# Memory values copied by two engines in halves, and a new order of VectorE, ScalarE and GpSimd work at the middle boundary of a two-block transformer kernel

## The chip, the cores and the metric

The kernel runs on one core of a Trainium2 chip. A core has TensorE (PE) for matmuls, VectorE (DVE), ScalarE (ACT) and GpSimd (POOL) for everything else, SyncE (SP) for issuing transfers; products land in PSUM, which the kernel uses as eight banks of 128 x 512 floats. The metric is the device time of one execution in microseconds; the median of three runs before the change is 2526.79 us.

## The reference

Two blocks follow each other on 256 tokens of width 2048. What matters here is how one ends and the other begins, and the memory attention in the first.

```python
def mem_cross_attention(x, mem, w_q, w_kv, w_o):
    q = (x @ w_q).reshape(B, S, N_HEADS_MEM, HEAD_DIM)
    k, v = jnp.split(mem @ w_kv, 2, axis=-1)
    s = jnp.einsum('bshd,bmhd->bhsm', q, k) * (HEAD_DIM ** -0.5)
    p = jax.nn.softmax(s, axis=-1)
    o = jnp.einsum('bhsm,bmhd->bshd', p, v).reshape(B, S, MEM_WIDTH)
    return o @ w_o

def first_block(x, mem, ...):
    ...
    y = mem_cross_attention(x, mem, w_q_mem, w_kv_mem, w_o_mem)
    x = layer_norm(ALPHA * x + y, ln_g[1], ln_b[1])
    y = swiglu(x, w_ffn_in, w_ffn_out)
    return layer_norm(ALPHA * x + y, ln_g[2], ln_b[2])

def second_block(x, c, ...):
    mod = jax.nn.silu(c) @ w_ada + b_ada
    h = modulate(rms_norm_2(x, norm1_w), shift1, scale1)
    p = h @ w_in
    ...
```

At the middle boundary the rows of x therefore pass through a layer norm (first root), and their result through an RMS norm (second root), before the first product of the second block, `lstm_q`, can begin.

## The kernel before

All weights come as one stream of 1 MB tiles through four buffers `raw`. ScalarE rounds each half tile to `whi`, VectorE subtracts to get `wlo`, and TensorE makes three matmuls for each product (hi x hi, hi x lo, lo x hi), at line 2215 with weights stationary, at 2219, 2258 and 2305 with the tokens stationary. TensorE is thus fed by ScalarE and VectorE with two halves in hand; each engine works strictly through its own instruction list, which is written out by hand, and waits on counting semaphores.

**Memory values.** The product `v_mem` fills one pair of PSUM banks: bank t holds the 128 memory rows of tile t and 512 columns, 128 for each of four heads. ScalarE waits for the product's end (`weights_used`) and copies both banks to `vm` in one instruction (line 757, by `read_out_rows`). TensorE waits for it (`pair_read`), and then multiplies `vm` by the transposed scores of each head (`mem_pT`) at line 2525; ScalarE and VectorE split the four results into `shi` (line 1032) and `slo` (line 1766) for the next product `o_mem`. VectorE's half tile at line 1521 stands ahead of the `slo`.

**The middle boundary.** `down1` ends with row tile 0's four banks, then row tile 1's (`last_four`). For each bank of 512 columns VectorE adds the residual and sums (`add_bank`, line 1620), and ScalarE squares and sums (`edge_square`, 670). From the sums come mean, variance and, by ScalarE's `root` (701) and VectorE's four small steps of `scale_from_root` (1675 to 1682), a scale. VectorE multiplies by `gamma` (`widen`, 1838) and then scales and adds `beta` (`normalise`, 1845). ScalarE squares the normed rows (`normed_squares`, 682), VectorE makes their mean (`mean_square`, 1664 to 1669), and a second root and scale follow. Row tile 0 is scaled by ScalarE (`scaled_rows`, 696), row tile 1 by VectorE (1833). Both are needed by TensorE's transposes (2155), then `lstm_q` begins (2215). While TensorE has nothing to do it multiplies a block of ones (`keep_busy`, 2143): 51 such matmuls here, of 512 columns, that nobody reads.

The counts tell which step is meant: `edge_var` and `edge_root` count 3 and 4 for row tile 0's two roots, 5 and 6 for row tile 1's. `scale_ready` counts every scale that VectorE has made, in the order in which it makes them. GpSimd, at the boundary, starts two transfers (572, 573), sets two tiles (574, 575) and makes four triangular masks (580) as soon as `down1` is done; they are needed by the gates and the heads of `lstm`, well into the second block.

## Time and profile before

| | us |
|---|---|
| median of three runs (2526.73 to 2526.83) | 2526.79 |
| the profiled execution | 2526.35 |
| its span, first to last instruction | 2524.7 |
| TensorE busy in it | 2504.4 |
| VectorE, ScalarE, GpSimd busy | 1670.4, 1247.2, 107.6 |
| memory values, `v_mem` to `o_mem` | 719.0 to 723.5 |
| middle boundary, end of `down1` to start of `lstm_q` | 1473.3 to 1487.7 |

The profile is of one execution. A timeline row gives start and duration in us from the span's start, the engine, the line of the kernel, the operation, the tile written and those read, shape, and the number of instructions that the row merges; a bracket tells how long the engine was idle before and what released it. Since engines overlap, what counts is which chain of waits sets TensorE's next start. A TensorE that is busy with the blocks of ones counts as busy in the table and does nothing for the result.

### The profile page before, as it was taken

What the parts mean: (1) busy time and instruction counts of PE and PEld (TensorE: products, weight loads), DVE (VectorE), ACT (ScalarE), POOL (GpSimd) and SP (SyncE); (2) the same over time, 40 slices, a digit from 0 to 9 for tenths busy, and PEclk for the clock granted to TensorE, in tenths of its full rate; (3) what the DMA queues carried; (4) which work ended last, traced back from release to release, by engine and by line L of the source; (5) the groups of instructions that cost most, each with busy time, mean ns of one, the idle gap of its engine ahead of it and who ended that gap; (6) DMA issues with size and microseconds to landing.
All of it is one profiled execution on the core that took longest, in us unless ns stands there. A gap on an engine that the chain in (4) does not pass through costs nothing.

```text
span 2524.7 us, 45946 instructions
## 1 busy us (share of the span) xinstructions
PE 2504.4 (99%) x17995; PEld 2327.2 (92%) x17999; DVE 1670.4 (66%) x2084; ACT 1247.2 (49%) x1588; POOL 107.6 (4%) x151
## 2 busy tenths in 40 slices
PE   9999999999999999999999999999999999999998
PEld 9799999998979999999988878988899999998886
DVE  5564675467867777777777775575766666665556
ACT  5444554444564444344444464545655555554444
POOL 0000000000100000000122000000000000000000
PEclk9999999999999999999999999999999999999999
DMA  7455445569647888888978736445455555555553
GB/s 304 154 199 186 157 146 193 187 256 362 256 157 299 332 344 329 343 330 339 363 285 330 259 135 214 167 149 216 167 187 197 193 190 199 186 196 209 190 198 118
DMA packets 82066, 581.95 MB, mean 230 GB/s; under 512 B 9308, under 2 KB 9468, under 8 KB 12096
## 3 DMA queue, kind: packets, MB, share of 16 engines
q1 hardware_dynamic: 65232, 462.98, 50.0%
q0 software_dynamic: 14464, 104.23, 10.6%
q10 hardware_dynamic: 2288, 13.59, 1.3%
q8 instruction: 58, 0.95, 0.2%
q14 instruction: 24, 0.20, 0.0%
HBM read 578.64 MB, written 2.12 MB: 230 GB/s over the span
## 4 chain that ended last, share of the span: by engine, by line
PE 96%; DVE 2%; issue 1%; ACT 1%; POOL 0%; DVEq 0%; ACTq 0%; POOLq 0%
PE ps L2215 60%; PE ps L2258 23%; PE ps L2219 7%; PE ps L2305 3%; PE ps L2283 0%; PE ps L2155 0%; PE ps L2576 0%; PE ps L2143 0%; PE ps L2417 0%; POOL small L539 0%; DVE wlo L1249 0%; PE ps L2450 0%; PE ps L2462 0%; DVE res L1838 0%; DVE res L1845 0%
## 5 line engine op out<-in xcount | busy, mean ns | idle before, releaser
L1249 DVE TENSOR_TENSOR wlo<-raw,whi 128x1024 fp32r<-128x1024 f32 x853 | 1034.0, 1227 | 659.8 <-ACT whi L633 655.9
L633 ACT ACTIVATE whi<-raw 128x1024 fp32r<-128x1024 f32 x850 | 891.3, 1060 | 961.2 <-PE ps L2215 595.0
L2215 PE MATMUL ps<-xhi,whi 128*128 128x256 f32 x4176 | 1155.4, 277 | 1.8 <-issue 1.8
L2215 PE MATMUL ps<-xhi,wlo 128*128 128x256 f32 x4176 | 1149.8, 275 | 0.0
L2215 PE MATMUL ps<-xlo,whi 128*128 128x256 f32 x4176 | 1149.6, 275 | 0.0
L2215 PEld LDWEIGHTS ps<-xhi,whi 128*128 128x128 f32 x4176 | 784.1, 188 | 4.0 <-issue 3.2
L2215 PEld LDWEIGHTS ps<-xlo,whi 128*128 128x128 f32 x4176 | 784.2, 188 | 0.4
L2215 PEld LDWEIGHTS ps<-xhi,wlo 128*128 128x128 f32 x4176 | 784.0, 188 | 0.0
L1313 DVE SCALAR_TENSOR_TENSOR ada<-ada,cb 128x2048 f32<-128x2048 f32 x96 | 219.5, 2286 | 2.7 <-DMA ada<-in_w_ada 2.7
L2258 PE MATMUL ps<-wlo,dhi 128*128 128x512 f32 x624 | 192.2, 389 | 0.0
L2258 PE MATMUL ps<-whi,dlo 128*128 128x512 f32 x624 | 192.1, 389 | 0.0
L2258 PE MATMUL ps<-whi,dhi 128*128 128x512 f32 x624 | 192.0, 389 | 0.0
L2258 PEld LDWEIGHTS ps<-whi,dlo 128*128 128x128 f32 x624 | 117.1, 188 | 24.5
L2258 PEld LDWEIGHTS ps<-wlo,dhi 128*128 128x128 f32 x624 | 117.1, 188 | 24.3
L2258 PEld LDWEIGHTS ps<-whi,dhi 128*128 128x128 f32 x624 | 117.1, 188 | 24.1
L2219 PE MATMUL ps<-whi,xhi 128*128 128x512 f32 (+1 forms) x224 | 87.9, 392 | 0.0
L2219 PE MATMUL ps<-whi,xlo 128*128 128x512 f32 (+1 forms) x224 | 85.8, 383 | 0.0
L2219 PE MATMUL ps<-wlo,xhi 128*128 128x512 f32 (+1 forms) x224 | 85.8, 383 | 0.0
L554 POOL DMA_DIRECT2D ada<-in_w_ada x94 | 50.2, 534 | 808.5 <-DVE ada L1313 790.7
L2073 DVE SCALAR_TENSOR_TENSOR conv<-ps,col,conv 128x255 f32<-128x255 f32 x176 | 72.7, 475 | 17.2 <-ACT conv L1182 17.2
L2215 PE MATMUL ps<-ohi,whi 128*128 128x256 f32 x256 | 70.6, 276 | 0.1
L2215 PE MATMUL ps<-ohi,wlo 128*128 128x256 f32 x256 | 70.4, 275 | 0.0
(374 smaller groups left out, 2179.0 us busy)
## 6 DMA issues: line engine op xcount, KB each, us to landing
raw<-in_stream SPq DMA_DIRECT2D x435, 1024.0 KB, 4.8
ada<-in_w_ada POOLq DMA_DIRECT2D x96, 1024.0 KB, 6.7
raw<-in_stream SPq DMA_DIRECT2D x5, 512.0 KB, 9.3
mem_part<-in_memt ACTq DMA_DIRECT2D x2, 1024.0 KB, 6.7
res<-in_x ACTq DMA_DIRECT2D x1, 2048.0 KB, 12.7
gamma<-in_ln_g ACTq DMA_DIRECT2D x2, 1024.0 KB, 9.8
beta<-in_ln_b ACTq DMA_DIRECT2D x2, 1024.0 KB, 14.0
gate_row<-gate_store POOLq DMA_DIRECT2D x2, 1024.0 KB, 7.7
```

The costliest lines, as they stand in the source:

```text
L554: pool.dma_start(ada[s % 2][:], w_ada[at(n0 + s, i, per)]).then_inc(ada_landed[s % 2], 16)
L633: act.activation(whi[:, h % 4], raw[g % 4][:, 1024 * half:1024 * half + 1024], ACT.Copy)\
L1249: dve.tensor_tensor(wlo[:, h % 4], raw[g % 4][:, 1024 * half:1024 * half + 1024], whi[:, h % 4].bitcast(F32), ALU.subtract).then_inc(lo_re ...
L1313: dve.scalar_tensor_tensor(out=ada[slot][:], in0=ada[slot][:], scalar=1.0, in1=cb[:], op0=ALU.mult, op1=ALU.mult, accum_out=mod[:, bass.ds ...
L2073: ins = dve.scalar_tensor_tensor(out=conv[:, q, S * m + to:S * m + to + S - 1], in0=bank[:, S * m + fro:S * m + fro + S - 1], scalar=col[: ...
L2215: ins = pe.matmul(o, w[:, k, P * m:P * m + P], a(kt), start=begins and n == 0 and m % 2 == 0, stop=ends and n == 2, skip_group_check=True)
L2219: ins = pe.matmul(o, a(kt)[:, P * m:P * m + P], w[:, k, :], start=begins and n == 0, stop=ends and n == 2, skip_group_check=True)
L2258: ins = pe.matmul(ps[:, 4 * t + 2 * half + n], a[:, s, P * t:P * t + P], w[:, h % 4, 512 * n:512 * n + 512], start=first and a is hi and w ...
L2305: return pe.matmul(ps[:, 4 * t + n], a[:, s, P * t:P * t + P], w[:, 512 * (n % 2):512 * (n % 2) + 512], start=begins and s == 0 and m == 0 ...
```

## The change

It has two parts. First, `vm` is copied by two engines, each one bank (one tile of memory rows), each in two halves of two heads: ScalarE makes `vm[:, 0]`, VectorE `vm[:, 1]`, placed behind VectorE's rest of the last weight tile and ahead of its half tile for `o_mem`. TensorE waits for the first halves ahead of head 0 and for the second halves ahead of head 2.

Second, at the middle boundary, VectorE takes row tile 1's third bank ahead of row tile 0's second mean square, and its fourth bank ahead of row tile 0's second scale; that scale moves behind row tile 1's `normalise`. ScalarE squares row tile 1's second and third bank ahead of row tile 0's second root and waits for the fifth scale, where it waited for the fourth, ahead of `scaled_rows`. The rest of the first weight half is made in two quarters. GpSimd's transfers and masks wait until row tile 1's scaled rows are done (`chunk_ready[1]` at 8), and the 51 matmuls on ones become 46.

```diff
@@ GpSimd
             pool.wait_ge(weights_used, through(AT["lstm_q"] - 1))
+            pool.wait_ge(chunk_ready[1], 8)
             pool.dma_start(dftc[:], dft).then_inc(late_landed, 16)
@@ ScalarE
-            read_out_rows(CH["v_mem"], g0 + 3, vm[:])
+            act.wait_ge(weights_used, through(g0 + 3))
+            c = CH["v_mem"]
+            act.activation(vm[:, 0, 0:S], ps[:, 2 * (c % 2), 0:S], ACT.Copy).then_inc(first_vm, 1)
+            act.activation(vm[:, 0, S:2 * S], ps[:, 2 * (c % 2), S:2 * S], ACT.Copy).then_inc(pair_read[c % 2], 1)
             wide_start("o_mem")
@@ ScalarE, middle boundary
             normed_squares(0)
+            edge_squares(1, 1, 1, 3)
             root(0, 4)
-            edge_squares(1, 1, 1, 4)
+            edge_squares(1, 1, 3, 4)
             second_upper_of_next(g0)
             root(1, 5)
-            scaled_rows(4)
+            scaled_rows(5)
             normed_squares(1)
@@ VectorE
-            def scale_from_root(t, count):
+            def scale_from_root(t, count, scaled=None):
...
-                dve.wait_ge(scale_ready, count)
+                dve.wait_ge(scale_ready, count if scaled is None else scaled)
@@ VectorE, memory values
             rest(g0 + 4)
+            dve.wait_ge(weights_used, through(g0 + 3))
+            c = CH["v_mem"]
+            for d in range(2):
+                dve.tensor_copy(vm[:, 1, S * d:S * d + S], ps[:, 2 * (c % 2) + 1, S * d:S * d + S]).then_inc(second_vm, 1)
             more_rest("o_mem", 1, (0,))
@@ VectorE, middle boundary
+            def rest_of_quarter(g, quarter):
+
+                cols = slice(512 * quarter, 512 * quarter + 512)
+                dve.wait_ge(hi_ready, 2 * g + 1)
+                return dve.tensor_tensor(wlo[:, 2 * g % 4, cols], raw[g % 4][:, cols], whi[:, 2 * g % 4, cols].bitcast(F32), ALU.subtract)
...
             add_bank(1, 1, 1, g0 - 1)
+            add_bank(1, 1, 2, g0 - 1)
             mean_square(0, 17)
-            scale_from_root(0, 4)
-            add_bank(1, 1, 2, g0 - 1)
             add_bank(1, 1, 3, g0 - 1)
             mean(1, 1)
             widen(1, 0, 13)
+            off_centre(1)
             widen(1, 1, 18)
-            off_centre(1)
             centred_variance(1, 20)
-            widen(1, 2, 20)
-            scale_from_root(1, 5)
+            widen(1, 2, 19)
+            scale_from_root(1, 5, 4)
             widen(1, 3, 20)
             normalise(1)
-            rest(g0, halves=(0,))
+            scale_from_root(0, 4, 5)
+            rest_of_quarter(g0, 0)
+            rest_of_quarter(g0, 1).then_inc(lo_ready, 1)
             mean_square(1, 24)
@@ TensorE
-            pe.wait_ge(pair_read[CH["v_mem"] % 2], reads(CH["v_mem"]))
+            pe.wait_ge(first_vm, 1)
+            pe.wait_ge(second_vm, 1)
             for h in range(HEADS_MEM):
+                if h == 2:
+                    pe.wait_ge(pair_read[CH["v_mem"] % 2], reads(CH["v_mem"]))
+                    pe.wait_ge(second_vm, 2)
                 pe.wait_ge(m_pT, h + 1)
...
-            first_chunk(4, "lstm_q", xn, 17, 51)
+            first_chunk(4, "lstm_q", xn, 17, 46)
```

What stands in a row at the places that the prediction speaks of follows. In these rows `ps` is PSUM, `edge` the small sums and scales, `res` the residual rows, `xn` the scaled rows, and a bracket names the semaphores that an instruction waits for.

VectorE at the middle boundary, from row tile 1's second bank on, before:

```order
L1620 SCALAR_TENSOR_TENSOR res,edge<-res,ps 128x512 [waits bank_done]
L1664 TENSOR_REDUCE edge<-edge 128x1 [waits edge_sq]
L1666 TENSOR_SCALAR edge<-edge 128x1 [waits dve_order]
L1669 SCALAR_TENSOR_TENSOR edge<-edge 128x1 [waits edge_sq,dve_order]
L1675 TENSOR_SCALAR edge<-edge 128x1 [waits edge_var]
L1677 RECIPROCAL edge<-edge 128x1 [waits edge_root]
L1679 SCALAR_TENSOR_TENSOR edge<-edge 128x1 [waits dve_order]
L1682 SCALAR_TENSOR_TENSOR edge<-edge 128x1 [waits dve_order]
L1620 SCALAR_TENSOR_TENSOR res,edge<-res,ps 128x512 [waits bank_done,scale_ready]
L1627 TENSOR_REDUCE edge<-edge 128x1 [waits added]
L1620 SCALAR_TENSOR_TENSOR res,edge<-res,ps 128x512 [waits weights_used]
```

The same place now:

```order
L1627 SCALAR_TENSOR_TENSOR res,edge<-res,ps 128x512 [waits bank_done] x2
L1634 TENSOR_REDUCE edge<-edge 128x1 [waits added]
L1671 TENSOR_REDUCE edge<-edge 128x1 [waits edge_sq]
L1673 TENSOR_SCALAR edge<-edge 128x1 [waits dve_order]
L1676 SCALAR_TENSOR_TENSOR edge<-edge 128x1 [waits edge_sq,dve_order]
L1627 SCALAR_TENSOR_TENSOR res,edge<-res,ps 128x512 [waits weights_used]
```

The third bank moved ahead of the mean square, and the four small steps of the scale are gone from in front of the fourth bank.

VectorE at the end of row tile 1's first norm, before:

```order
L1845 SCALAR_TENSOR_TENSOR res<-res,edge,beta 128x512 [waits dve_order]
L1845 SCALAR_TENSOR_TENSOR res<-res,edge,beta 128x512 x3
L1249 TENSOR_TENSOR wlo<-raw_50,whi 128x1024 [waits hi_ready]
L1664 TENSOR_REDUCE edge<-edge 128x1 [waits edge_sq]
L1666 TENSOR_SCALAR edge<-edge 128x1 [waits dve_order]
```

And now:

```order
L1862 SCALAR_TENSOR_TENSOR res<-res,edge,beta 128x512 [waits dve_order]
L1862 SCALAR_TENSOR_TENSOR res<-res,edge,beta 128x512 x3
L1682 TENSOR_SCALAR edge<-edge 128x1 [waits edge_var]
L1684 RECIPROCAL edge<-edge 128x1 [waits edge_root]
L1686 SCALAR_TENSOR_TENSOR edge<-edge 128x1 [waits dve_order]
L1689 SCALAR_TENSOR_TENSOR edge<-edge 128x1 [waits dve_order]
L1845 TENSOR_TENSOR wlo<-raw_50,whi 128x512 [waits hi_ready,scale_ready]
L1845 TENSOR_TENSOR wlo<-raw_50,whi 128x512 [waits hi_ready]
L1671 TENSOR_REDUCE edge<-edge 128x1 [waits edge_sq]
L1673 TENSOR_SCALAR edge<-edge 128x1 [waits dve_order]
```

Row tile 0's second scale, the four rows from L1682, now stands behind the four rows of `normalise`.

ScalarE at the middle boundary, from row tile 0's normed squares on, before:

```order
L682 ACTIVATE ps,edge<-res 128x512 [waits normed0] x4
L701 ACTIVATE edge<-edge 128x1 [waits edge_var]
L670 ACTIVATE ps,edge<-res,edge 128x512 [waits added] x3
L706 ACTIVATE whi<-raw_50 128x1024 [waits weights_used]
L701 ACTIVATE edge<-edge 128x1 [waits edge_var]
L696 ACTIVATE xn<-res,edge 128x512 [waits scale_ready]
L696 ACTIVATE xn<-res,edge 128x512 x3
L682 ACTIVATE ps,edge<-res 128x512 [waits normed1] x4
L701 ACTIVATE edge<-edge 128x1 [waits edge_var]
```

And now:

```order
L685 ACTIVATE ps,edge<-res 128x512 [waits normed0] x4
L673 ACTIVATE ps,edge<-res,edge 128x512 [waits added] x2
L704 ACTIVATE edge<-edge 128x1 [waits edge_var]
L673 ACTIVATE ps,edge<-res,edge 128x512 [waits added]
L709 ACTIVATE whi<-raw_50 128x1024 [waits weights_used]
L704 ACTIVATE edge<-edge 128x1 [waits edge_var]
L699 ACTIVATE xn<-res,edge 128x512 [waits scale_ready]
L699 ACTIVATE xn<-res,edge 128x512 x3
L685 ACTIVATE ps,edge<-res 128x512 [waits normed1] x4
L704 ACTIVATE edge<-edge 128x1 [waits edge_var]
```

The first root moved behind two squares; the scaled rows still stand ahead of row tile 1's normed squares.

## Rows read from the trace of the kernel before

**Rows 1.** The profile's page, part 1: busy time, share of the span, instructions.

```profile
PE 2504.4 (99%) x17995; PEld 2327.2 (92%) x17999; DVE 1670.4 (66%) x2084; ACT 1247.2 (49%) x1588; POOL 107.6 (4%) x151
```

**Rows 2.** Waits of TensorE over the span: total us, times, longest.

```profile
PE ps L2155 <- DVE xn L1833: 2.6, 2, 1.4
...
PE ps L2215 <- DVE small L1592: 1.6, 1, 1.6
...
PE ps L2525 <- ACT vm L757: 1.1, 1, 1.1
```

**Rows 3.** Timeline of the memory values, start us, us, engine, line, operation.

```profile
719.01 1.02 ACT L757 ACTIVATE vm<-ps 128x1024 f32<-128x1024 f32 x1 [2.15 <-PE ps L2219]
...
720.09 3.72 PE L2525 MATMUL ps<-mem_pT,vm 128*128 128x256 f32 x16 [1.11 <-ACT vm L757]
721.01 1.23 DVE L1521 TENSOR_TENSOR more_lo<-raw,more_hi_o_mem 128x1024 fp32r<-128x1024 f32 x1 [6.15 <-ACT more_hi_o_mem L917]
721.26 0.38 ACT L1032 ACTIVATE shi<-ps 128x256 fp32r<-128x256 f32 x1 [0.28 <-PE ps L2525]
```

**Rows 4.** Groups by line and shape: busy us, mean ns of one, idle before.

```profile
L1344 DVE COPY ckv<-ps 128x512 f32<-128x512 f32 x1 | 0.7, 680 | 0.0
...
L1147 ACT ACTIVATE fa_late<-ps 128x256 f32<-128x256 f32 x4 | 1.5, 376 | 4.1 <-PE ps L2615 4.1
```

**Rows 5.** Timeline of VectorE over the middle boundary.

```profile
1466.08 0.15 DVE L1644 TENSOR_TENSOR edge<-edge 128x1 f32<-128x1 f32 x1
...
1466.97 0.68 DVE L1620 SCALAR_TENSOR_TENSOR res<-res,ps 128x512 f32<-128x512 f32 x1
...
1473.98 0.68 DVE L1620 SCALAR_TENSOR_TENSOR res<-res,ps 128x512 f32<-128x512 f32 x1
...
1474.95 1.42 DVE L1838 SCALAR_TENSOR_TENSOR res<-res,edge,gamma 128x512 f32<-128x512 f32 x2
1476.28 0.35 DVE L1644 TENSOR_TENSOR edge<-edge 128x1 f32<-128x1 f32 x1
...
1477.60 0.74 DVE L1838 SCALAR_TENSOR_TENSOR res<-res,edge,gamma 128x512 f32<-128x512 f32 x1
1478.26 0.14 DVE L1675 TENSOR_SCALAR edge<-edge 128x1 f32<-128x1 f32 x1
...
1478.96 0.75 DVE L1838 SCALAR_TENSOR_TENSOR res<-res,edge,gamma 128x512 f32<-128x512 f32 x1
...
1482.40 1.22 DVE L1249 TENSOR_TENSOR wlo<-raw,whi 128x1024 fp32r<-128x1024 f32 x1
...
1483.91 0.16 DVE L1669 SCALAR_TENSOR_TENSOR edge<-edge 128x1 f32<-128x1 f32 x1
...
1484.98 1.67 DVE L1833 TENSOR_SCALAR xn<-res,edge 128x512 f32<-128x512 f32 x4
```

**Rows 6.** Timeline of ScalarE over the same stretch.

```profile
1477.82 2.54 ACT L696 ACTIVATE xn<-res,edge 128x512 f32<-128x512 f32 x4
1480.53 0.60 ACT L682 ACTIVATE ps<-res 128x512 f32<-128x512 f32 x1 [0.16 <-DVE res L1845]
...
1483.05 0.19 ACT L682 ACTIVATION_READ_ACCUMULATOR ps<-res 128x1 f32 x1
```

**Rows 7.** Timeline of GpSimd over the same stretch: its four masks.

```profile
1475.80 1.67 POOL L580 TENSOR_SCALAR_AFFINE_SELECT tri<-tri 128x256 f32<-128x256 f32 x4
```

**Rows 8.** Timeline of TensorE over the same stretch.

```profile
1473.35 10.83 PE L2143 MATMUL ps<-warm 128*128 128x512 bf16 x49
1485.62 1.06 PE L2155 MATMUL ps<-ident,xn 128*128 128x128 f32 x8 [1.44 <-DVE xn L1833]
...
1487.70 0.35 PE L2215 MATMUL ps<-xhi,whi 128*128 128x256 f32 x1 [0.58 <-issue]
```

**Rows 9.** TensorE's matmuls on ones at launch: duration ns min/median/max, first and last start.

```profile
L2143 PE MATMUL ps<-warm x5: 607/634/634, 1.2 to 2.9; 128*128 128x512 bf16 x5
```

**Rows 10.** The same line in the window 6.5 to 8.3 us.

```profile
L2143 PE MATMUL ps<-warm x8: 378/380/634, 6.3 to 8.3; 128*128 128x512 bf16 x8
```

More of the change, by code:

```diff
@@ L376, in two_blocks @@
         first_T = sem("first_T")
+        first_vm = sem("first_vm")
+        second_vm = sem("second_vm")
         first_odd = sem("first_odd")
@@ L1828, in _, with scaled_rows @@
             dve.wait_ge(ln_landed, 96)
-            def scaled_rows():
-                for k in range(4):
+            def rest_of_quarter(g, quarter):
+                cols = slice(512 * quarter, 512 * quarter + 512)
+                dve.wait_ge(hi_ready, 2 * g + 1)
+                return dve.tensor_tensor(wlo[:, 2 * g % 4, cols], raw[g % 4][:, cols], whi[:, 2 * g % 4, cols].bitcast(F32), ALU.subtract)
+            def scaled_rows(k0=0, k1=4):
+                for k in range(k0, k1):
                     dve.tensor_scalar(xn[:, 1, cut(k)], res[:, 1, cut(k)], scale_of(1), None, ALU.mult).then_inc(chunk_ready[1], 1)
```

## The prediction

> **What bounds the kernel now.** I read the busy times first. TensorE is busy for 2504.4 of 2524.7 us [rows 1], so only what makes it wait, or work on something else, can give time back. The view of waits comes next. It shows how short TensorE's waits for others are: 1.1 us ahead of the memory values, 1.4 us at the middle boundary, and a longest of 1.6 [rows 2]. The busy time hides one thing. At the middle boundary TensorE is busy from 1473.35 with matmuls on ones [rows 8], and does nothing useful until its transposes at 1485.62. So the boundary's true wait is 12.3 us, and what sets it is the chain of VectorE and ScalarE, which the timelines of these two engines show in order [rows 5, 6]. In that chain the last steps are: VectorE's `normalise` of row tile 1 (the next instruction starts at 1482.40), ScalarE's normed squares of that tile (1480.53 to 1483.24), VectorE's mean square and scale (last step of the mean at 1483.91), and the scaled rows at 1484.98. TensorE follows 0.64 us later.
>
> **Memory values.** Before, ScalarE copies 1024 columns in 1.02 us from 719.01, and TensorE starts at 720.09 after 1.11 us of waiting [rows 3]. Now TensorE needs 256 columns of each engine. ScalarE's copy of that shape from PSUM took 376 ns [rows 4]. VectorE's copy of 256 columns isn't in the trace. A copy of 512 columns took 680 ns [rows 4], which bounds it from above; from below I take 340 ns, half of that. The value I use is 0.43, since a fixed part doesn't halve. VectorE has been idle for 6.15 us when it starts its next half tile [rows 3], so it can start with ScalarE at 719.01. TensorE then starts at 719.01 + 0.43 + 0.06 (the lag between copy and matmul before: 720.09 - 719.01 - 1.02) = 719.50, that is 0.59 us earlier; with the bounds 0.34 to 0.69. The second halves end by 719.9, while heads 0 and 1 take half of the 3.4 us of these matmuls, so they hide.
>
> What follows must move up too. ScalarE ends its copies at about 719.7 where it ended at 720.03, so its half tile, 1.05 us, ends at 720.7, and the first `shi`, at 721.26 before [rows 3], can start at 720.7: 0.56 us earlier. VectorE's half tile follows it as before. TensorE has three more heads to do before it needs the first `slo`, which covers this. From there on the work is driven by TensorE until the first boundary, and all of it moves. I put this part at **-0.6 us**.
>
> **The middle boundary, VectorE's first part.** Row tile 1's fourth bank is added at 1473.98 before [rows 5], though TensorE had finished by 1473.35, when its matmuls on ones begin [rows 8]. With the scale's four small steps taken out ahead of it, VectorE waits for TensorE there: 0.63 us earlier. ScalarE's squares come in time for what follows: each takes under 0.8 us, and the fourth one, released at about 1474.0, ends at 1474.9, well ahead of the variance at 1476.
>
> Next, the masks. The small steps of row tile 1 from line 1644 to the next wide instruction took 1.32 us (1476.28 to 1477.60), while GpSimd made its masks (1475.80 to 1477.47) [rows 5, 7]; the same steps of row tile 0 took 0.89 us (1466.08 to 1466.97) [rows 5]. Moving the masks gives 0.43 us. The wide instruction at line 1838 wasn't slower beside them: two took 1.33 us from start to next start, at 1474.95, in part beside the masks. The Trainium skill (GPSIMD Engine Reference, Specifications) says that GpSimd shares its SBUF interfaces with VectorE and contends with VectorE instructions that have two SBUF inputs. By that rule the wide ones should be slowed and not only the small ones; the row shows the small ones slowed, and the sum goes by the row. So VectorE's `normalise` of row tile 1 ends at 1482.40 - 0.63 - 0.43 = 1481.34, **1.06 us earlier**. If nothing else had changed, this is what the boundary would gain.
>
> **The middle boundary, ScalarE's wait.** But row tile 0's second scale is now made behind `normalise`. Its four small steps take 0.70 us (1478.26 to 1478.96) [rows 5], so it is ready at 1481.34 + 0.70 = 1482.04. ScalarE waits for it: `scaled_rows` asks for the fifth scale, and the fifth is now this one. Behind that wait, on ScalarE's queue, stand row tile 0's four scaled rows and then row tile 1's normed squares. Before, the scaled rows ran from 1477.82, right behind the root of row tile 1, and were done in 2.54 us, so that the squares could follow `normalise` piece by piece [rows 6]. Now ScalarE idles from about 1476.8 (1477.82, earlier by the same 1.06 us) to 1482.04, makes the scaled rows until 1482.04 + 2.54 = 1484.58, and then the squares, which took 2.71 us (1480.53 to 1483.24): 1487.29. VectorE's last step of the mean follows at 1487.33, and the scaled rows of row tile 1 come 1.07 us behind it (1483.91 to 1484.98) [rows 5]: 1488.40. That is 3.42 us later than before. Instructions of one engine overlap by some hundredths, so I take **+3.4 us**, with 3.0 to 3.6 as its bounds. VectorE's two quarters (1.2 us before in one piece) lie in the 4 us in which it waits for the squares and cost nothing; they would cost 1.2 if the squares came in time.
>
> The transposes then start at 1489.0. The 46 matmuls on ones end at 1473.35 + 46 x 0.212 = 1483.1 (51 took 10.83 us; the row counts 49 of them, two are missing in the records) [rows 8]. TensorE is idle for **5.9 us**, more than three times its longest wait before, 1.6 us [rows 2].
>
> **The clock.** At launch a matmul on ones takes 634 ns, later 378 [rows 9, 10]. From the start of one to the next these are 0.43 us (1.2 to 2.9 in four steps) and, at the boundary, 0.21 [rows 8], 512 columns at 1.2 and at 2.4 GHz. The slow ones begin at 1.2 us and end soon behind 6.3, where the median of eight is fast already. So TensorE out of rest works at the lower level for some 5.5 us. What a rest of 5.9 us does in the middle, no row shows: waits up to 1.6 us left the matmuls at full rate, and the rest before launch didn't. The cost is between 0 and half of 5.5 us, 2.8. If the clock falls, the first 2.1 us behind the restart are spent on transposes and on waits for other engines (1485.62 to 1487.70) [rows 8] and lose little; the rest loses (5.5 - 2.1) / 2 = **+1.7 us**. The Trainium skill (TensorE: Matmul & The Clock Gate, HAM oscillation) holds that a pause of this kind between bursts of matmuls puts TensorE back to half rate, and that it must earn its full rate again; no run here shows it so far.
>
> **GpSimd's wait.** Its queue holds, behind the new wait, the two transfers, the tiles and the masks, some 3.6 us in all. They are needed by the gates of `lstm` behind a whole chunk, so they hide. But the masks now run at about 1491, beside the first chunk's splits, which have to keep ahead of TensorE. I take 0; were all of the 0.43 us to show, and again for the wide ones, 0.9.
>
> **The sum**, against the profiled execution of 2526.35 us: 2526.35 - 0.6 + 3.4 + 1.7 = 2530.85. The median of the runs is 0.44 above that execution, so 2531.3.
>
> **The rivals.**
> (A) The forecast: ScalarE's wait costs 3.4 us and the clock falls in the pause: 2531.3. For it: the order on ScalarE's queue is strict, and the pause is nearer to the rest before launch, behind which the rate was low, than to any of the short waits: that is where I chose, and not by much. Chance 0.45.
> (B) The clock doesn't fall: 2529.6. For it: every wait that the trace has, up to 1.6 us, left the rate alone. Chance 0.37.
> (C) The masks collide with the first chunk as well, or the clock takes its full 2.8 us: between 2532.2 and 2533.3. Against it: the first chunk's engines are not full, and at half rate they have more time. Chance 0.10.
> (D) The time falls. The mechanism is ScalarE's release: if row tile 0's rows are scaled in the gap behind the root, from 1476.8 to 1479.3, and the squares follow `normalise`, only the 1.06 us counts, less the four small steps of 0.70 that now stand behind `normalise`: -0.35, with the memory values -0.95, and 2525.8. It decides this way if the fifth scale is ready before about 1478.6, 3.4 us ahead of where I put it. Against it: by the order of VectorE's queue the scale stands behind `normalise`. Chance 0.05.
> (E) The memory values gain nothing, since VectorE's copy is slow or o_mem's halves are late, and the rest is as in A or B: 0.6 more than those. Chance 0.03.
>
> **How the numbers follow.** The likeliest is A, 2531.3. The range 2528.8 to 2532.8 holds A, B and E with the bounds of the wait and the clock, and half of C. It leaves out D. A measurement of this kernel can tell 0.2%, about 5.05 us, from no change: slower by that is above 2531.84. C and a quarter of A (clock cost over 2.2 us) are there: 0.10 + 0.11, with E 0.22. Faster by over 0.2% needs 5 us, which no term has: 0.01. The remaining 0.77 is within 0.2%.
>
> **What would show it.** In the trace after: TensorE's first matmul on `vm` about 0.5 us behind the last one of `v_mem`, with two copies of 0.4 us beside each other; row tile 1's fourth bank added right at TensorE's end; the small steps of row tile 1 as fast as row tile 0's; a ScalarE idle of about 5 us behind the root, ended by VectorE's scale; the four scaled rows and only then the squares; TensorE idle for 5 to 6 us ahead of the transposes. Whether the clock fell shows in the duration of the two matmuls on ones behind the transposes and of the first ones of `lstm_q`: 634 and not 378 ns for the former. The prediction is wrong if ScalarE's idle is short, or if the small steps are still slow. It would be wrong in size if the first halves of `lstm_q` wait for VectorE's splits.

## The result

| | before | after |
|---|---|---|
| median of 20 runs, us | 2526.66 | 2530.71 |
| spread of the runs, us | 2526.29 to 2526.83 | 2529.91 to 2531.79 |
| profiled execution, us | 2526.35 | 2530.69 |
| its span, us | 2524.7 | 2529.1 |
| mean granted clock | 0.999 | 0.998 |

The ratio of the times is 1.0017, with a 95% interval of 1.001 to 1.0023. The change costs 4.05 us by the medians, 0.16%, where the prediction had 4.5 (2531.3 for 2526.79). That is inside what it called "within 0.2%". The runs of after also spread over 1.9 us, those of before over 0.5.

### The profile page after: what moved, and what is told of

It reads as the page before. It is cut to its first block, busy times and chain, and to the rows that moved or that the text cites. A ratio compares the mean times of both kernels' runs of the same rounds, so it can differ in the third digit from the quotient of the medians.

```text
span 2529.1 us, 45945 instructions
## 1 busy us (share of the span) xinstructions
PE 2505.2 (99%) x17994; PEld 2328.8 (92%) x17994; DVE 1670.5 (66%) x2087; ACT 1246.4 (49%) x1589; POOL 109.1 (4%) x151
## 4 chain that ended last, share of the span: by engine, by line
PE 96%; DVE 2%; ACT 1%; issue 1%; POOL 0%; DMA 0%; DVEq 0%; ACTq 0%; POOLq 0%
PE ps L2233 60%; PE ps L2276 23%; PE ps L2237 7%; PE ps L2323 3%; PE ps L2173 0%; PE ps L2301 0%; PE ps L2598 0%; PE ps L2435 0%; POOL small L541 0%; DVE wlo L1256 0%; PE ps L2468 0%; PE ps L2480 0%; PE ps L2474 0%; DMA xT<-in_xt 0%; ACT whi L636 0%
```

## The profile after

The first view is the page's busy times; they answer to [rows 1] and hide the loss in the same way, since TensorE's share stays at 99%.

```profile
PE 2505.2 (99%) x17994; PEld 2328.8 (92%) x17994; DVE 1670.5 (66%) x2087; ACT 1246.4 (49%) x1589; POOL 109.1 (4%) x151
```

TensorE's waits (total us, times, longest) answer to [rows 2]. The wait for `xn` at the boundary is the only one that grew by more than 0.3 us, from 1.4 to 5.8. The one for `vm` fell from 1.1 to 0.6.

```profile
PE ps L2173 <- DVE xn L1850: 7.0, 2, 5.8
...
PE ps L2233 <- DVE small L1599: 1.6, 1, 1.6
...
PE ps L2547 <- ACT vm L1031: 0.6, 1, 0.6
```

**The memory values.** These are the timelines of ScalarE, VectorE and TensorE there (start us, us, engine, line, operation; the bracket is the idle time ahead and what ended it). They answer to [rows 3]: both engines start their copies together, the first two take 0.38 us, and TensorE starts 0.52 us behind the start of the copies, where it was 1.08 (720.09 - 719.01). That is 0.56 of the 0.62 us between the two traces (719.47 for 720.09); the other 0.06 us lie ahead of anything that was changed.

```profile
718.95 0.38 ACT L1031 ACTIVATE vm<-ps 128x256 f32<-128x256 f32 x1 [2.15 <-PE ps L2237]
```
```profile
718.95 0.76 DVE L1773 COPY vm<-ps 128x256 f32<-128x256 f32 x2 [4.15 <-PE ps L2237]
```
```profile
719.47 1.75 PE L2547 MATMUL ps<-mem_pT,vm 128*128 128x256 f32 x7 [0.56 <-ACT vm L1031]
```

**VectorE at the middle boundary**, to be read against [rows 5].

```profile
1472.63 0.69 DVE L1627 SCALAR_TENSOR_TENSOR res<-res,ps 128x512 f32<-128x512 f32 x1 [0.27 <-PE ps L2323]
...
1478.22 2.74 DVE L1862 SCALAR_TENSOR_TENSOR res<-res,edge,beta 128x512 f32<-128x512 f32 x4
1480.88 0.15 DVE L1682 TENSOR_SCALAR edge<-edge 128x1 f32<-128x1 f32 x1
...
1481.38 0.16 DVE L1689 SCALAR_TENSOR_TENSOR edge<-edge 128x1 f32<-128x1 f32 x1
1481.57 1.29 DVE L1845 TENSOR_TENSOR wlo<-raw,whi 128x512 fp32r<-128x512 f32 x2
1486.00 0.16 DVE L1671 TENSOR_REDUCE edge<-edge 128x1 f32<-128x3 f32 x1 [3.13 <-ACT ps L685]
...
1487.76 1.67 DVE L1850 TENSOR_SCALAR xn<-res,edge 128x512 f32<-128x512 f32 x4
```

The fourth bank now follows TensorE's end at once, and `normalise` is done at 1480.88. The second scale of row tile 0 stands behind it and is ready at 1481.5. Then come the two quarters, and then VectorE idles for 3.13 us, until ScalarE's squares.

**ScalarE over the same stretch**, against [rows 6].

```profile
1481.57 2.56 ACT L699 ACTIVATE xn<-res,edge 128x512 f32<-128x512 f32 x4 [5.41 <-DVE edge L1689]
1484.04 0.58 ACT L685 ACTIVATE ps<-res 128x512 f32<-128x512 f32 x1
...
1486.39 0.19 ACT L685 ACTIVATION_READ_ACCUMULATOR ps<-res 128x1 f32 x1
```

This is the loss in three lines: 5.41 us of waiting for a scale of four small steps, then the scaled rows, and only behind them the squares for which the whole boundary waits. Before, the scaled rows were made from 1477.82 and the squares from 1480.53.

**TensorE over the same stretch**, against [rows 8].

```profile
1472.20 0.39 PE L2323 MATMUL ps<-whi,dlo 128*128 128x512 f32 x1
1472.44 10.19 PE L2161 MATMUL ps<-warm 128*128 128x512 bf16 x46
1488.40 1.94 PE L2173 MATMUL ps<-ident,xn 128*128 128x128 f32 x8 [5.77 <-DVE xn L1850]
1490.13 1.06 PE L2161 MATMUL ps<-warm 128*128 128x512 bf16 x2
1490.72 0.68 PE L2233 MATMUL ps<-xhi,whi 128*128 128x256 f32 x1
...
1493.12 0.41 PE L2233 MATMUL ps<-xlo,whi 128*128 128x256 f32 x1
...
1493.62 0.28 PE L2233 MATMUL ps<-xlo,whi 128*128 128x256 f32 x1
...
1494.92 0.60 PE L2173 MATMUL ps<-ident,xn 128*128 128x128 f32 x4
```

Two things are to be seen. TensorE idles for 5.77 us. And behind it the clock is at the lower of its two levels, 1.2 GHz: the granted clock is 1.00 until 1486.6, 0.50 from there to 1493.4, and 1.00 again; the same eight transposes take 1.94 and not 1.06 us, and products of `lstm_q` take 0.41 and not 0.28. So the clock fell in the pause, 1.8 us ahead of its end, and came back about 5 us behind it. The Trainium skill (TensorE: Matmul & The Clock Gate, HAM oscillation) says that a pause between bursts, if it lasts long enough, puts TensorE back to half rate; the trace agrees here, with 5.77 us.

The difference can be split at three marks of the two traces. Before, two of them are these rows, the end of `down1` and the transposes of block 2:

```profile
1472.89 0.39 PE L2305 MATMUL ps<-whi,dlo 128*128 128x512 f32 x1
...
1490.54 0.60 PE L2155 MATMUL ps<-ident,xn 128*128 128x128 f32 x4
```

The last `down1` matmul ends 0.69 us earlier (1472.59 for 1473.28). The transposes start 15.81 us behind it, where it was 12.34: +3.47. From there to the transposes of block 2 it is 6.52 us (1488.40 to 1494.92), where it was 4.92 (1485.62 to 1490.54): +1.60, which `ones_73` below shows to be the clock. Only 0.24 of it lies ahead of `lstm_q`'s first product (2.32 us for 2.08), 1.36 behind. The sum, +4.38, is the difference of the two spans, 4.4.

## The experiments

Each time is a median of 11 runs, and a difference is against 33 runs of before on the same chip (medians 2526.61, 2526.69 and 2526.56). Where two of the kernels are compared, each goes by its own median. The intervals are wide against most of these differences: only those of `ones_73`, `scale_only` and `middle_only` leave out 1. For the smaller ones the traces have to carry the reading.

**The clock by itself, 1: a pause and nothing else.** Before, with fewer matmuls on ones at the boundary.

```
-            first_chunk(4, "lstm_q", xn, 17, 51)
+            first_chunk(4, "lstm_q", xn, 17, 30)
```

> The kernel before with 30 matmuls on ones where it has 51: TensorE's pause ahead of the middle transposes grows from 1.4 to about 5.9 us, and no other engine's work changes. Theory (a pause of this length alone throws the clock down): the transposes start at the same time, the first half of lstm_q is slow, about 1.6 us above the kernel before. Rival (the clock has to do with something else in the change): no difference.

Measured: 2528.17, +1.56, ratio 1.0007 (0.9998 to 1.0016), with runs from 2526.9 to 2528.67. The transposes start as before, 12.32 us behind the end of `down1` for 12.34, so the pause costs by the clock alone.

```profile
1485.46 1.94 PE L2155 MATMUL ps<-ident,xn 128*128 128x128 f32 x8 [5.78 <-DVE xn L1833]
...
1488.27 0.41 PE L2215 MATMUL ps<-xlo,whi 128*128 128x256 f32 x1
...
1488.67 0.28 PE L2215 MATMUL ps<-xhi,whi 128*128 128x256 f32 x1
```

This profiled execution was the cheapest of the eleven, 0.55 us above the profiled execution of before, and it was back at full rate by 1488.67, 3.2 us behind the pause instead of 5. The clock fell at about 1481.8 here, 3.7 us ahead of the transposes, and 1.8 us ahead of them in after. So how much of the low rate falls on work depends on when it sets in and ends, and from the transposes to those of block 2 this trace lost 0.68 us (5.60 for 4.92) where after lost 1.60. That would explain the spread of after, and the next experiment bears it out.

**The clock by itself, 2: after without the pause.**

```
-            first_chunk(4, "lstm_q", xn, 17, 46)
+            first_chunk(4, "lstm_q", xn, 17, 73)
```

> The changed kernel with 73 matmuls on ones where it has 46, so that TensorE stays busy through its 5.8 us pause; nothing else differs. Theory (the clock fell in the pause): the transposes come as in the changed kernel, the two matmuls on ones behind them take 378 ns each, lstm_q's first matmuls are at full rate, and 1.6 us come back: about 2.4 us above the kernel before. Rival (the slow first half of lstm_q is VectorE's and GpSimd's collision): it stays slow, 4.0 us above the kernel before.

Measured: 2529.66 (2529.5 to 2529.93), +2.97, ratio 1.0011 (1.0002 to 1.002). The spread shrinks from 1.9 to 0.4 us.

```profile
1472.84 16.07 PE L2161 MATMUL ps<-warm 128*128 128x512 bf16 x73
1488.81 1.06 PE L2173 MATMUL ps<-ident,xn 128*128 128x128 f32 x8
1489.71 0.60 PE L2161 MATMUL ps<-warm 128*128 128x512 bf16 x2
1490.89 0.36 PE L2233 MATMUL ps<-xhi,whi 128*128 128x256 f32 x1 [0.58 <-issue]
```

No slow stretch is left. From the end of `down1` to the transposes of block 2 it is 20.73 us, against 22.33 in after: 1.60, the clock's term in the trace. By the medians it is 1.05. I had put the result at 2.4 above before; it is 2.97. The boundary did give back the 1.60 of after's trace, but the two spans differ by only 1.1: the profiled execution of `ones_73` began its copies of `vm` at 719.36 and that of after at 718.95, 0.41 us apart ahead of anything in which they differ. What the clock costs in the typical execution of after is therefore known only as 1.0 to 1.6 us.

**The wait by itself: before with nothing but the late scale.** In ScalarE's order `scaled_rows(4)` becomes `scaled_rows(5)`; the helper gets the count it needs; on VectorE:

```
             mean_square(0, 17)
-            scale_from_root(0, 4)
...
-            scale_from_root(1, 5)
+            scale_from_root(1, 5, 4)
             widen(1, 3, 20)
             normalise(1)
+            scale_from_root(0, 4, 5)
```

> The kernel before with row tile 0's second scale moved behind row tile 1's normalise, and ScalarE's scaled rows waiting for the fifth scale; banks, masks, 51 ones and memory values as before. Theory: normalise ends about 0.7 us earlier (the fourth bank no longer waits for the four small steps), ScalarE idles until 0.7 behind it, the transposes come 3.8 us later than before, and the pause of 5.2 us may or may not throw the clock down (1.6 us): 3.8 to 5.4 us above the kernel before. Rival (the wait isn't the cause): within 0.5 us of before.

Measured: 2531.55, +4.94, ratio 1.0019 (1.001 to 1.0028). One moved block of four small steps makes the whole loss and more. TensorE waits as in after, and the clock falls as well, 0.8 us ahead of the transposes; the profiled execution is the slowest of the eleven, and loses 2.04 us from there to block 2 (6.96 for 4.92).

```profile
1489.32 1.94 PE L2155 MATMUL ps<-ident,xn 128*128 128x128 f32 x8 [4.99 <-DVE xn L1833]
```

The masks stay where they were in before, and VectorE comes to them earlier, so they lie beside one of its wide instructions, which took 0.75 us without them:

```profile
1476.78 0.96 DVE L1838 SCALAR_TENSOR_TENSOR res<-res,edge,gamma 128x512 f32<-128x512 f32 x1
```

**The masks alone.** Before with GpSimd's new wait.

```
             pool.wait_ge(weights_used, through(AT["lstm_q"] - 1))
+            pool.wait_ge(chunk_ready[1], 8)
             pool.dma_start(dftc[:], dft).then_inc(late_landed, 16)
```

> The kernel before with GpSimd's wait for row tile 1's scaled rows alone. Theory: the small steps of row tile 1 take 0.89 us where they took 1.32, the transposes come 0.4 us earlier, and lstm_q at full rate has room for the masks: 0.4 us below the kernel before. Rival (the masks beside the first chunk's splits, which took 0.89 for 0.69 and 1.30 for 1.22 us there, hold TensorE up): the gain is cancelled or turned, 0 to 0.5 us above.

Measured: 2526.16, -0.45, ratio 0.9999 (0.999 to 1.0008). Row tile 1's small steps take 0.94 us to the next wide instruction, where they took 1.32 in [rows 5]. The masks now lie beside the first chunk:

```profile
1476.23 0.15 DVE L1645 TENSOR_TENSOR edge<-edge 128x1 f32<-128x1 f32 x1
...
1477.17 0.75 DVE L1839 SCALAR_TENSOR_TENSOR res<-res,edge,gamma 128x512 f32<-128x512 f32 x1
```
```profile
1489.01 0.89 DVE L1281 TENSOR_TENSOR xlo<-modulated,xhi 128x512 fp32r<-128x512 f32 x1
1489.82 1.30 DVE L1250 TENSOR_TENSOR wlo<-raw,whi 128x1024 fp32r<-128x1024 f32 x1
```
```profile
1488.78 2.86 POOL L581 TENSOR_SCALAR_AFFINE_SELECT tri<-tri 128x256 f32<-128x256 f32 x4
```

They do collide there. In before, without masks beside them, the same two splits were faster:

```profile
1489.43 0.69 DVE L1280 TENSOR_TENSOR xlo<-modulated,xhi 128x512 fp32r<-128x512 f32 x1
1490.04 1.22 DVE L1249 TENSOR_TENSOR wlo<-raw,whi 128x1024 fp32r<-128x1024 f32 x1
```

And the masks took 1.67 us where they lay in before [rows 7], for 2.86 here. But no wait of TensorE appears behind it, and the gain is what was counted.

**The memory values alone, and the boundary alone.** The first is before with the halves; the second is after with ScalarE's one copy instead. ScalarE's part of the edit, which one has and the other lacks, with VectorE's and TensorE's counterparts as in the change:

```
-            read_out_rows(CH["v_mem"], g0 + 3, vm[:])
+            act.wait_ge(weights_used, through(g0 + 3))
+            c = CH["v_mem"]
+            act.activation(vm[:, 0, 0:S], ps[:, 2 * (c % 2), 0:S], ACT.Copy).then_inc(first_vm, 1)
+            act.activation(vm[:, 0, S:2 * S], ps[:, 2 * (c % 2), S:2 * S], ACT.Copy).then_inc(pair_read[c % 2], 1)
```

> The kernel before with the first part alone (memory values by two engines in halves). Theory: TensorE waits 0.56 us ahead of the values where it waited 1.11, and the whole rest moves: 0.55 to 0.65 us below the kernel before. Rival: the gain is lost at a later boundary, no difference above 0.2 us.

Measured: 2526.11, -0.58, ratio 0.9997 (0.9988 to 1.0006).

> The kernel before with the second part of the change alone (middle boundary, masks, 46 ones); the memory values are copied in one piece as before. Theory (the parts add up): 4.0 + 0.6 = 4.6 us above the kernel before. Rival (the vm part gives nothing in the end, its gain being taken back later): 4.0 us above.

Measured: 2531.02, +4.33, ratio 1.0017 (1.0008 to 1.0026). I had put it at 4.6, or 4.0 if the first part gave nothing; it lies between. The two parts sum to +3.75, and after has +4.05. The 0.3 us between them is less than what the fallen clock makes the runs differ by, so by the medians the tenths stay open. The traces are sharper on the first part: from the start of the copy of `vm` to the end of `down1` it is 754.21 to 754.27 us in the five traces with one copy, and 753.63 to 753.70 in the nine with halves.

**Which release undoes it? First: squares ahead.** In after, ScalarE makes row tile 1's squares and root first, and the rows of tile 0 behind them.

```
             root(1, 5)
-            scaled_rows(5)
             normed_squares(1)
             root(1, 6)
+            scaled_rows(5)
```

> The changed kernel with ScalarE's order turned: row tile 1's normed squares and its second root ahead of row tile 0's scaled rows. Theory (ScalarE's wait for the fifth scale holds up the squares): the squares follow normalise, VectorE's mean comes right behind its two quarters, at about 1483.0, the transposes at about 1484.7, TensorE's pause falls to about 2 us and the clock stays; in all 0.9 to 1.5 us below the kernel before. Rival (the squares' place doesn't matter, VectorE's own queue is late): no gain on the changed kernel, about 4.0 us above before.

Measured: 2526.73, +0.04, ratio 1.0002 (0.9993 to 1.0012). So 4.0 us of the 4.05 are gone, the clock's part among them: the loss was the order of ScalarE's queue. The 0.9 to 1.5 below before that I expected did not come, for three reasons. The mean square still stands behind the two quarters on VectorE, and the transposes follow VectorE's first scaled row by 0.63 us, as they do by 0.63 or 0.64 in every trace here (the bracket below names ScalarE's, but the first of those was done by 1484.5). Against the end of `down1` they start after 12.27 us, where before had 12.34 and 12.1 was expected:

```profile
1481.33 0.60 ACT L685 ACTIVATE ps<-res 128x512 f32<-128x512 f32 x1
...
1483.69 0.20 ACT L704 ACTIVATE edge<-edge 128x1 f32<-128x1 f32 x1 [1.64 <-DVE edge L1676]
1483.80 2.54 ACT L699 ACTIVATE xn<-res,edge 128x512 f32<-128x512 f32 x4
```
```profile
1481.91 1.29 DVE L1845 TENSOR_TENSOR wlo<-raw,whi 128x512 fp32r<-128x512 f32 x2
...
1484.58 1.67 DVE L1850 TENSOR_SCALAR xn<-res,edge 128x512 f32<-128x512 f32 x4
```

Next, ScalarE is busy with its late rows until 1486.3 and comes to the first block of `lstm_q` only then, so the first product starts 2.60 us behind the transposes, for 2.08 in before (it is 2.60 in `squares_56` below too, where the clock did not fall).

And the executions fall into two groups: six between 2526.49 and 2526.73, one at 2527.28, and four between 2528.72 and 2529.14, these with a mean clock of 0.997 and not 0.999. The profiled one is of the upper group:

```profile
1485.21 1.06 PE L2173 MATMUL ps<-ident,xn 128*128 128x128 f32 x8 [2.24 <-ACT xn L699]
1486.11 0.69 PE L2161 MATMUL ps<-warm 128*128 128x512 bf16 x2
1487.81 0.55 PE L2233 MATMUL ps<-xhi,whi 128*128 128x256 f32 x1 [1.01 <-issue]
1488.15 0.41 PE L2233 MATMUL ps<-xlo,whi 128*128 128x256 f32 x1
```

The transposes are still at full rate; the clock falls only behind them. The granted clock is 1.00 until about 1486.5 and 0.50 from there to 1493.3. So two waits of 2.24 and 1.01 us, close together, seem to be enough in some executions and not in others.

**Is it the waits?** The same with ten more matmuls on ones, 56 for 46.

```
-            first_chunk(4, "lstm_q", xn, 17, 46)
+            first_chunk(4, "lstm_q", xn, 17, 56)
```

> The kernel squares_ahead with 56 matmuls on ones where it has 46, which closes its pause of 2.2 us ahead of the transposes. Its executions fell in two groups, about 2526.6 and 2528.7 to 2529.1. Theory (a pause of 2.2 us with one of 1.0 behind it throws the clock down in some executions): only the lower group is left, 2526.5 to 2526.8. Rival (the upper group has another cause, a transfer for instance): both groups appear again.

Measured: 2526.53 (2526.3 to 2526.78), -0.03, ratio 1.0 (0.9991 to 1.0009). The upper group is gone, none of eleven for four or five of eleven, and the median is where the lower group was. The wait of 2.24 us is gone in this trace, and the one behind the transposes, 1.10 us, is still there: so it takes the first one. From the transposes to those of block 2 it is 5.45 us here and 7.85 in the profiled execution of `squares_ahead`; the 2.40 us between them are what the two groups differ by.

**Second: the scale early again.** After, with row tile 0's second scale ahead of the fourth bank.

```
             mean_square(0, 17)
+            scale_from_root(0, 4)
             add_bank(1, 1, 3, g0 - 1)
...
             normalise(1)
-            scale_from_root(0, 4, 5)
```

> The changed kernel with one thing undone: row tile 0's second scale is made where it was, ahead of row tile 1's fourth bank, and ScalarE's scaled rows wait for the fourth scale again; everything else (memory values, bank order, masks, quarters, 46 ones) as in the changed kernel. Theory (the place of this scale is the whole loss): normalise ends 0.4 us later than in the changed kernel, at about 1481.3, the squares follow it, the transposes come at about 1484.6, TensorE's pause is about 1.5 us and the clock stays: 1.2 to 1.6 us below the kernel before, in all 5.2 to 5.6 below the changed one. Rival (the new bank order or the quarters cost as well): at or above the kernel before.

Measured: 2526.22, -0.34, ratio 0.9999 (0.999 to 1.0008), which is 4.5 us below after. (One execution of 4148 us at a mean clock of 0.567 is left out of this; nothing here tells its cause.) The direction is right, the gain too small: I had expected 1.2 to 1.6 below before. The scale now waits for ScalarE's root, which stands behind two of the edge squares, and the fourth bank starts only at 1474.04, 0.87 us behind the end of `down1` (1473.17) where it was 0.70 before; `normalise` is done 9.09 us behind that end, for 9.12 in before:

```profile
1473.39 0.16 DVE L1684 RECIPROCAL edge<-edge 128x1 f32<-128x1 f32 x1 [0.26 <-ACT edge L704]
...
1474.04 0.69 DVE L1627 SCALAR_TENSOR_TENSOR res<-res,ps 128x512 f32<-128x512 f32 x1
```

So with the banks' order of after the scale can stand ahead of the fourth bank or behind `normalise`, and each place costs something, but the first 4.5 us less, the clock's part included.

**Third: the split behind the scale too.** After, with squares ahead on ScalarE, and on VectorE the mean square right behind the scale:

```
             scale_from_root(0, 4, 5)
-            rest_of_quarter(g0, 0)
-            rest_of_quarter(g0, 1).then_inc(lo_ready, 1)
             mean_square(1, 24)
             scale_from_root(1, 6)
-            scaled_rows()
+            scaled_rows(0, 1)
+            rest_of_quarter(g0, 0)
+            rest_of_quarter(g0, 1).then_inc(lo_ready, 1)
+            scaled_rows(1, 4)
```

(`squares_first` is the kernel that is called `squares_ahead` above.)

> The kernel squares_first with VectorE's two quarters of the first weight half moved from ahead of row tile 1's second mean to behind the first of its scaled rows. Theory: the squares of row tile 1 end 0.7 us behind normalise, so the two quarters (1.2 us) were partly on the path there; now the mean comes about 1 us earlier, the transposes at about 1483.9, and TensorE's start of lstm_q is set by VectorE's quarters and splits: 1.5 to 2.3 us below the kernel before. Rival (lstm_q waits for the first weight half instead): no gain on squares_first.

Measured: 2525.71 (2525.58 to 2526.21), -0.90, ratio 0.9997 (0.9988 to 1.0006), where I had expected 1.5 to 2.3 below. The transposes start at 1483.71, but the first product comes only 3.1 us behind them, since VectorE does three more scaled rows (1.27 us) ahead of the first splits of `xn`:

```profile
1483.71 1.06 PE L2174 MATMUL ps<-ident,xn 128*128 128x128 f32 x8 [1.03 <-ACT xn L699]
...
1486.84 0.35 PE L2234 MATMUL ps<-xhi,whi 128*128 128x256 f32 x1 [1.63 <-issue]
```

**Fourth: the rows that nobody waits for go later.** On top of `rest_later`, scaled rows 1 to 3 of VectorE and 2 and 3 of ScalarE are made inside the first chunk, behind its first splits.

```
                    .then_inc(xlo_ready, 1)
+                if rows is not None:
+                    rows(1, 2)
                 rest(g, halves=(1,))
                 x_rest_scaled(n, 1)
+                if rows is not None:
+                    rows(2, 4)
```

> The kernel rest_later with row tile 1's scaled rows 1 to 3 moved on VectorE behind the first splits of lstm_q's first chunk, where TensorE needs them, and ScalarE's third and fourth scaled rows of row tile 0 behind its split of block 2. Theory (lstm_q's first product waited 1.6 us for these rows' queues): TensorE's first product starts about 1.1 us earlier than in rest_later, at about 1485.7: 1.8 to 2.1 us below the kernel before. Rival (the rows, now in the first chunk, make its later halves late): no gain on rest_later, 0.9 below before.

Measured: 2524.65 (2524.33 to 2525.03), -1.91, ratio 0.9993 (0.9984 to 1.0002). It is faster than both kernels, 6.1 us below after. By itself it is still within 0.2% of before, but the slowest run of it is 1.2 us faster than the fastest of before.

```profile
1483.53 1.06 PE L2179 MATMUL ps<-ident,xn 128*128 128x128 f32 x8 [1.05 <-ACT xn L699]
...
1485.61 0.36 PE L2239 MATMUL ps<-xhi,whi 128*128 128x256 f32 x1 [0.58 <-issue]
```

**Fifth: both ideas together.** `scale_early` with VectorE's late rows as in the last one, and the second quarter behind the first scaled row.

```
             rest_of_quarter(g0, 0)
-            rest_of_quarter(g0, 1).then_inc(lo_ready, 1)
             mean_square(1, 24)
             scale_from_root(1, 6)
-            scaled_rows()
+            scaled_rows(0, 1)
+            rest_of_quarter(g0, 1).then_inc(lo_ready, 1)
```

> The kernel scale_early with VectorE's second quarter moved behind the first scaled row of row tile 1, and its scaled rows 1 to 3 behind the first splits of the first chunk; ScalarE's scaled rows are done long before. Theory: the first product starts at about 1486, 1 us earlier than in scale_early: 2.0 to 2.4 us below the kernel before. Rival: the first chunk's later halves come late, no gain on scale_early.

Measured: 2525.41 (2524.91 to 2525.66), -1.15, ratio 0.9995 (0.9986 to 1.0005). It gains 0.8 over `scale_early` but keeps its late fourth bank, and is 0.8 behind `rows_later`. I had expected the best of all, 2.0 to 2.4 below before; the step that failed is the same as in `scale_early` (fourth bank 0.88 us behind the end of `down1`).

## Why the prediction was right

The mechanism was the predicted one at each step: the late scale, ScalarE's idle, the rows ahead of the squares, the pause and the fallen clock. That the sum came so close is in part luck, since small misses cancel in it. Point by point, in its own steps:

- **Memory values, -0.6.** -0.58 with this part alone, and 753.69 us for 754.27 from the copies to the end of `down1` in its trace. VectorE's copy of 256 columns took 0.38 us in both halves, for the 0.43 that was taken; the lag from the copy to the first matmul was 0.14 us (718.95 + 0.38 to 719.47) for 0.06, which took the gain back. So the 0.59 us were right in part by two small errors that cancel.
- **VectorE's first part, 1.06 us earlier.** `normalise` is done at 1480.88, 8.29 us behind the end of `down1`, where it was 9.12: only 0.83. The fourth bank gained its 0.66 (0.04 us behind TensorE's end for 0.70). From its start to the end of `normalise` it was 8.42 us and is 8.25: 0.17 for the 0.43 of the masks. The masks themselves did give 0.45 in `masks_only`, 0.38 of it in these steps. What took back most of the rest is the new order of the small steps, which I had costed at nothing: they now stand in two groups between wide instructions, 0.44 and 0.68 us, 1.12 in all, where `masks_only` has 0.94 in one. No run has the new order alone, so this is read from the traces.
- **ScalarE's wait, +3.4.** +3.47 in the trace, and every link is there in the order named: scale behind `normalise`, rows 2.56, squares, mean, rows 1.67. ScalarE's idle was 5.41 where 5.2 was worked out (1476.8 to 1482.04). From the end of `normalise` to the transposes it took 7.52 us for my 7.70, since squares that follow one another behind the rows take 0.58 and not 0.60 us and nothing lies between; that made up for the 0.23 lost in the step above. `scale_only` shows the mechanism alone. The rival D, that the rows slip into the gap behind the root, did not happen; where the scale was made early, in `scale_early`, it was 0.34 below before where D had 0.95, since VectorE's first part gained nothing there.
- **The clock, +1.7.** +1.60 in the trace, 1.56 by `before_ones30`, 1.05 by `ones_73` against after. This was the choice between A and B, and the one that no row of before could settle. It was decided rightly, from the rest before launch being the nearest row, but with 0.45 against 0.37 it was near to a guess, and the size had luck in it. The 5.5 us of low rate, taken from launch, were 5.0 behind the pause in this execution and 3.2 in another; and the first 2.1 us, taken to lose little, lost 0.24. The traces lost between 0.68 and 2.04 us behind a long pause, by when the clock fell and came back.
- **Masks beside the first chunk, 0.** The collision is real (splits 0.69 to 0.89 and 1.22 to 1.30 us, masks 3.10), larger than I had reason to think, and still costs TensorE nothing: with the clock kept up, `ones_73` has 4.92 us from the transposes to those of block 2, as before. The Trainium skill's rule (GPSIMD Engine Reference, Specifications) is that GpSimd contends with VectorE instructions of two SBUF inputs. These rows agree. So do the small steps of before, which I had read as slowed one and all: of the five, the two that were slow are L1644 (0.35 us for 0.15) and L1654 (0.33 for 0.16), both with two SBUF inputs. The wide L1838 of before, with two as well, ran beside the masks unslowed, in part; but in `scale_only`, where the masks fell on the third one, it took 0.96 us for 0.75. So such instructions are slowed in some places and not in others, and what decides it the runs don't settle.
- **The size.** 4.5 predicted, 4.05 measured. The three terms sum to 4.38 in the traces, 0.1 under the prediction. The rest is the step from the traces to the medians: the profiled execution of after is at its median (2530.69 for 2530.71), and that of before is 0.31 below its own, where the prediction had taken 0.44 for both kernels.

The misses are in the experiments. `ones_73` was 0.6 us too low, as told there. The others are on the way back: three times (`squares_ahead`, `rest_later`, `scale_early`) I took away the wait that ended last and gave it back in full, without working out which wait ended next: ScalarE's first block of `lstm_q` behind its scaled rows, VectorE's first splits behind scaled rows, the root behind edge squares. `rows_later` was worked out from the trace of the one before it, and hit.

## What to carry to other kernels

A short step that another engine waits for must not be moved behind a long one, however little it costs itself: ask what is queued behind the waiter, here 2.5 us of rows and then the squares on which everything hung. Work of an engine is ordered by who waits for it, the chain first, and what only feeds later blocks behind it; with the same copies and banks that was worth 6.1 us here, of which 1.0 to 1.6 were the clock's. And if TensorE must pause for some us, matmuls on ones up to the end of the pause can be worth their trouble, since the pause was paid a second time by the clock: the 27 more in `ones_73` gave back 1.05 us.

## What was not expected of the hardware

- A pause of 5.0 to 5.8 us put the clock down in the profile of each of the four kernels with one (after, `before_ones30`, `scale_only`, `middle_only`), and the eight transposes took 1.94 us for 1.06. But also waits of 2.24 and 1.01 us did so in four or five of eleven executions, at a cost of 2.4 us, more than the 1.6 of after's long pause: here the low rate set in behind the transposes, and 5.5 us of it fell on `lstm_q`'s products, 2.7 in after (1490.7 to 1493.4), while 2.34 and 0.58 us (`scale_early`) and 1.03 and 1.63 (`rest_later`) left the profiled executions alone (two other runs of `scale_early` had a mean clock of 0.998). With before's 1.44 and 0.58 us no execution was over 2527.6.
- The low rate lasted between 3.1 us (`middle_only`) and 6.0 us (`scale_only`, until 1495.3) behind the pause, in kernels that do the same work there. It makes runs of one kernel differ, by 1.9 us in after and 2.65 in `squares_ahead`.
- GpSimd's masks took 1.24 us in `scale_only`, 1.67 in before, and 2.86 to 3.37 beside VectorE's splits of the first chunk. Of VectorE's instructions only some with two SBUF inputs were slowed beside them: two of the small steps in before, the wide L1838 in `scale_only` (0.96 us for 0.75), the splits in after (0.89 for 0.69 and 1.30 for 1.22). In `rest_later` the masks took 3.01 us and the splits beside them their usual 0.68 and 1.22. No small step with one SBUF input was slower.
